# Clipping the up projections of 32 experts on ScalarE in two rectified steps instead of on VectorE in one

## What is computed

```
gate = xb @ w_gate[e] + b_gate[e]
up = xb @ w_up[e] + b_up[e]
gate = jnp.minimum(gate, 7.0)
up = jnp.clip(up, -7.0, 7.0)
glu = gate * jax.nn.sigmoid(1.702 * gate)
return (glu * (up + 1.0)) @ w_down[e] + b_down[e]
```

## Time and profile before

| | us |
|---|---|
| median of three runs | 1713.48 |
| lowest and highest of them | 1712.59, 1715.12 |
| profiled execution | 1710.51 |
| its span in the trace | 1709.2 |
| TensorE busy in it | 1615.4 (95%) |
| VectorE busy in it | 1343.9 (79%) |
| ScalarE busy in it | 1196.1 (70%) |

### The profile page before, as it was taken

How to read it: one execution, slowest core, us unless ns; L and a number is a source line. 1 busy time by engine, 2 the same in 40 slices (tenths; PEclk the granted TensorE clock), 3 DMA queues, 4 the chain that set the end, 5 groups by cost and what they waited for, 6 DMA issues and landing times.

```text
span 1709.2 us, 19409 instructions
## 1 busy us (share of the span) xinstructions
PE 1615.4 (95%) x7465; PEld 1304.9 (76%) x7465; DVE 1343.9 (79%) x1032; ACT 1196.1 (70%) x931; POOL 238.7 (14%) x169
## 2 busy tenths in 40 slices
PE   6999977999999999999999999999978999999998
PEld 5877865877877877877877877877865877778886
DVE  4476688899999999999999999999986325865343
ACT  4354356888888888888888888888865256664232
POOL 1402028131120120120120120120000000000000
PEclk9999989999999999999999999999997999999999
DMA  8412287999999999999999999999974311113221
GB/s 289 132 50 74 91 287 288 389 407 413 413 408 416 412 409 416 409 410 410 409 410 409 410 410 407 406 410 407 392 291 153 123 50 60 64 56 123 90 72 50
DMA packets 96335, 483.85 MB, mean 283 GB/s; under 512 B 14616, under 2 KB 16336, under 8 KB 47088
## 3 DMA queue, kind: packets, MB, share of 16 engines
q1 hardware_dynamic: 81408, 458.45, 67.0%
q0 software_dynamic: 10624, 18.35, 4.2%
q10 hardware_dynamic: 4208, 5.77, 1.0%
HBM read 475.91 MB, written 23.51 MB: 292 GB/s over the span
## 4 chain that ended last, share of the span: by engine, by line
PE 75%; DVE 13%; ACT 7%; issue 4%; DMA 1%; ACTq 0%; SPq 0%; DVEq 0%
PE PS L546 66%; ACT WH L1048 5%; DVE low L1401 4%; DVE WL L1401 4%; PE PS L788 3%; PE PS L983 1%; DVE eu L1747 1%; DVE eu L1752 1%; PE PS L995 1%; PE PS L802 1%; PE PS L578 1%; DVE hl L1738 1%; DMA h2d<-HV 1%; PE PS L658 0%; PE PS L976 0%
## 5 line engine op out<-in xcount | busy, mean ns | idle before, releaser
L1048 ACT ACTIVATE WH<-land 128x2048 fp32r<-128x2048 f32 x210 | 396.6, 1912 | 139.7 <-PE PS L546 138.9
L1048 ACT ACTIVATE WH<-ring 128x2048 fp32r<-128x2048 f32 x218 | 411.9, 1913 | 92.8 <-PE PS L546 84.5
L1401 DVE TENSOR_TENSOR low<-ring,WH 128x2048 fp32r<-128x2048 f32 x194 | 437.2, 2286 | 22.4 <-ACT WH L1048 21.4
L1401 DVE TENSOR_TENSOR WL<-land,WH 128x2048 fp32r<-128x2048 f32 x190 | 427.7, 2286 | 23.5 <-ACT WH L1048 22.9
L2072 POOL DMA_INDIRECT accd<-ys,lists x29 | 61.2, 2109 | 774.3 <-ACT ys L1236 774.3
L546 PE MATMUL PS<-WH,xh 128*128 128x512 f32 x512 | 161.0, 396 | 3.7 <-DVE low L1401 2.9
L546 PE MATMUL PS<-WH,hh 128*128 128x512 f32 x512 | 149.2, 393 | 1.5 <-DVE hh L1736 1.5
L546 PE MATMUL PS<-WH,xs 128*128 128x512 f32 x512 | 144.3, 405 | 1.8 <-DVE xs L1736 1.8
L546 PE MATMUL PS<-WH,xl 128*128 128x512 f32 x512 | 137.3, 390 | 0.0
L1401 DVE TENSOR_TENSOR WL<-ring,WH 128x2048 fp32r<-128x2048 f32 x24 | 54.8, 2289 | 92.9 <-ACT WH L1048 92.9
L546 PEld LDWEIGHTS PS<-WH,xs 128*128 128x128 f32 x512 | 98.2, 195 | 21.9 <-issue 2.2
(11 more groups left out here) (423 smaller groups left out, 2947.9 us busy)
## 6 DMA issues: line engine op xcount, KB each, us to landing
land<-in_w_up_dram SPq DMA_DIRECT2D x71, 1024.0 KB, 9.1
ring<-in_w_down_dram SPq DMA_DIRECT2D x71, 1024.0 KB, 9.5
ring<-in_w_gate_dram SPq DMA_DIRECT2D x66, 1024.0 KB, 9.6
land<-in_w_gate_dram SPq DMA_DIRECT2D x62, 1024.0 KB, 10.2
ring<-in_w_up_dram SPq DMA_DIRECT2D x57, 1024.0 KB, 9.2
land<-in_w_down_dram SPq DMA_DIRECT2D x57, 1024.0 KB, 10.0
ring<-in_w_in_dram SPq DMA_DIRECT2D x19, 1024.0 KB, 5.7
land<-in_w_in_dram SPq DMA_DIRECT2D x13, 1024.0 KB, 5.2
```

The source lines that it names most:

```text
L1048: A.activation(WH[buf[n]], lands[spot[n]], ACT.Copy).then_inc(s_hi, 1)
L1401: V.tensor_tensor(WLn[n], lands[spot[n]], WH[buf[n]].bitcast(F32), SUB).then_inc(s_lo, 1)
```

## The change

`vector_up` goes away for all experts. In its place stands `scalar_up`: ScalarE reads the up sums from PSUM and writes `eu = relu(7 - up)`, waits for its own result, and writes `eu = relu(14 - eu)`, which is the clipped up plus 7. VectorE's product adds -6 instead of 1. A constant column with 14 is added to the constants, in a column that the load of constants covered already.

The places in the queues change too. For even experts from 2 to 30, `scalar_up(e)` stands in the loop of e itself, at item d3, ahead of the high part of g3 of the next expert, and `vector_glu(e)` moves one item forward, to the place that `vector_up` had. For odd experts and for expert 0, `scalar_up` stands in the next loop at item g0, behind the high part of g4, and `vector_glu` stays at item g1. For the last expert, 31, `scalar_up` stands ahead of `scalar_out(30)` and of the last `hh`.

```diff
+    c[:, LIM], c[:, LIM2] = 7.0, 14.0
...
+    def scalar_up(e):
+        if small(e):
+            A.wait_ge(s_fold, fold["up", e])
+        else:
+            A.wait_ge(s_mm, done[n_g[e, 7] + 1])
+        if e:
+            A.wait_ge(s_tt, t_mid[e - 1] + 1)
+        A.activation(eu, PS[:, 2:4, :], ACT.Relu, scale=-1.0, bias=C[:, LIM:LIM + 1]).then_inc(ac.sem, ac.one())
+        A.wait_ge(ac.sem, ac.n)
+        A.activation(eu, eu, ACT.Relu, scale=-1.0, bias=C[:, LIM2:LIM2 + 1]).then_inc(s_eu, 1)
...
             if e == E:
+                scalar_up(E - 1)
                 scalar_out(E - 2)
...
+                if (what, p) == ("d", 3) and 0 < e < E and not small(e):
+                    scalar_up(e)
                 high(ahead(n_g[e, p] if what == "g" else n_d[e - 1, p]))
+                if (what, p) == ("g", 0) and e and (small(e - 1) or e == 1):
+                    scalar_up(e - 1)
...
-        V.tensor_scalar(eu, PS[:, 2:4, :], 7.0, -7.0, MIN, MAX).then_inc(s_eu, 1)
...
-        V.scalar_tensor_tensor(eu, eu, 1.0, eg, ADD, MUL).then_inc(s_eh, 1)
+        V.scalar_tensor_tensor(eu, eu, -6.0, eg, ADD, MUL).then_inc(s_eh, 1)
...
-                vector_up(E - 1)
                 vector_glu(E - 1)
...
-                if (what, p) == ("g", 0) and e:
-                    vector_up(e - 1)
-                if (what, p) == ("g", 1) and e:
+                if (what, p) == ("g", 1 if small(e - 1) or e == 1 else 0) and e:
                     vector_glu(e - 1)
```

More of the change, by code:

```diff
@@ L21 @@
 KB = 1024
-IDENT, LTRI, TRII, ONES, CAUS, SEL4, RCP, TOKK, IOTA, IOT1, OVJ, EPS5, EPS6, LIM = 0, 128, 256, 384, 512, 640, 1152, 1216, 1232, 1264, 1392, 1395, 1396, 1397
+IDENT, LTRI, TRII, ONES, CAUS, SEL4, RCP, TOKK, IOTA, IOT1, OVJ, EPS5, EPS6, LIM, LIM2 = 0, 128, 256, 384, 512, 640, 1152, 1216, 1232, 1264, 1392, 1395, 1396, 1397, 1398
 NC1 = 1400
@@ L51, in constants @@
     c[:, EPS5], c[:, EPS6] = 1e-5, 1e-6
-    c[:, LIM] = 7.0
+    c[:, LIM], c[:, LIM2] = 7.0, 14.0
     late = c[:, NC1:]
```

## The result

| | median us | runs | lowest, highest |
|---|---|---|---|
| before | 1713.03 | 4 | 1710.72, 1715.12 |
| after | 1723.80 | 4 | 1723.49, 1724.57 |

The changed kernel takes 1.0068 times as long as the one before, with a 95% interval of 1.0056 to 1.008: 10.8 us slower. The forecast was 1725.4 us, 11.9 us slower. The profiled execution took 1723.87 us, with a span of 1722.6.

What follows compares the result with a forecast made beforehand. TensorE, busy 95%, was taken to bound the kernel, waiting on the ScalarE and VectorE chain to the product and `hl`; +16.0 - 1.0 - 1.1 - 2.0 = +11.9 us gave 1725.4 us, range 1721 to 1730 (8 in 10: 1712 to 1735).

Steps and rivals of the forecast that it cites:

- The deciding term: Even experts 2 to 30: ScalarE's 2.20 us delay `hl`, less VectorE's 1.13; 1.07 us lost in each of 15 pairs, +16.0 us.
- Odd experts at no cost: Odd experts 1 to 29: `scalar_up` at g0 fits its 2.20 us into ScalarE's waits; cost nothing.
- The ends: Experts 0 and 31: VectorE's chain gets shorter at 0, ScalarE is free at 31; -1.0 and -1.1 us.
- The clock: TensorE's falls to half clock behind the transposes, in 7 of 15 pairs, mostly do not come; -2.0 us.
- The rival with more falls: Waits around d0: the clock falls behind the `hh` wait and costs fully, 1735 to 1739 us; chance 13%.
- The sum: Whole kernel: +16.0 - 1.0 - 1.1 - 2.0 = +11.9 us, giving 1725.4 us.
- Busy times: Sign in the changed trace: ScalarE busy some 72 us longer, VectorE 39 us shorter.

Runs made afterwards that it cites:

- one-step run: Changed kernel with the second rectified step left out for even experts 2 to 30 (outputs not the reference's); 1707.73 us against 1711.37, ratio 0.9977.
- one-item-later run: Changed kernel with the even experts' two steps one item later, behind the high part of g4; 1721.03 us against 1711.37, ratio 1.0049.
- x6: Changed kernel with `hh` directly behind `egl` and `hl` ahead of the low part of g6, in odd experts' loops; 1705.78 us against 1711.71, ratio 0.9964.
- x8: Kernel before, all clips still on VectorE, only reordered: product, `hh` and `hl` earlier; 1702.05 us, ratio 0.9945.
- x9: Order of x8, loading only half the columns of d1 and d3 of experts 1 to 31 (outputs not the reference's); 1682.14 us against 1712.11, ratio 0.983.

## Why the prediction was right

**The deciding term.** Forecast: +1.07 us in each of 15 pairs, from 2.20 added on ScalarE and 1.13 taken off VectorE. Measured in an undisturbed pair: 65.00 - 63.96 = 1.04. Each link is in the rows above: the steps cost 2.20 us, VectorE's low part of g4 begins 8.67 us behind the released piece (forecast 8.7), the product's wait is 0.56 (0.6), `hh` 1.67 (1.9), `hl` 1.25 (1.5). The two waits were forecast 0.2 too long each and the end of the chain not: the forecast counted TensorE's work by its steps, while a wait is counted from the end of the last matmuls, 0.16 us beyond their step (1.07 against 0.91), and the first matmuls behind a wait take 0.73 us instead of 0.62. The one-step run shows that the delay counts one for one; the run with `hl` earlier shows that the chain ends at `hl`.

**Odd experts at no cost.** Right: ScalarE's timeline behind the fold is

```profile
568.04 1.10 ACT L1234 ACTIVATE eu<-PS,C 128x1024 f32<-128x1024 f32 x1
...
571.23 5.52 ACT L1048 ACTIVATE WH<-ring 128x2048 fp32r<-128x2048 f32 x3
577.89 1.92 ACT L1048 ACTIVATE WH<-ring 128x2048 fp32r<-128x2048 f32 x1 [1.14 <-PE PS L546]
```

The waits between the three high parts are filled, and the 1.14 us ahead of the fourth is still whole, as in the earlier trace rows.

**The ends.** Forecast -1.0 and -1.1. The start gave -1.9 in the trace: the group of the earlier trace rows's kind behind the first even expert comes at 359.30 instead of 360.13, with 1.04 of that pair's loss in it. Of it 0.3 us come from ahead of the experts (VectorE is 0.29 earlier at 250 us). The clip's part is 0.7 and not 1.0: the product begins at 273.80 instead of 274.79, these 0.3 included, since VectorE now waits 0.34 us for ScalarE's high part. The other 0.9 us arise between 283 and 346 us, where the stretches of half clock lie otherwise (two, at 283 and 293 us, before; a double one at 288 us after). That part was not in the forecast and is luck. The tail gave -1.1: from the last such group (1193.71 and 1204.70) to the transposes of expert 31 it is 80.04 us before and 79.97 after, with the last pair's 1.04 in it.

**The clock.** Forecast -2.0, since the falls would go. Right: 7 became none. The reason given, that the waits would be shorter or set apart, is supported by the one-item-later run, where one wait grew to 2.33 us and the falls came in nearly every pair. The rival with more falls named a mechanism that exists, as that run shows, but it needed a wait longer than 1.67 us.

**The sum.** Up to the second block's transposes the trace gives 1318.73 - 1307.19 = +11.5 us, forecast +11.9. The 15 pairs gave 13.9 of it (14 x 0.92 and 1.04 for the last, the clock's gain included; forecast 14.0), the ends -3.0 (forecast -2.1), and 0.6 arose between the last expert and the second block, which the forecast did not have. The second block then was 1.9 us longer in this execution, by the fall of the clock described above, so the span grew by 13.4, and the medians by 10.8. The pairs are what the forecast had worked out; that the whole came out within 1.1 us is in part luck, as the small terms cancel and single executions of before differ by 4.4 us.

**Busy times.** By their group the 64 new instructions of ScalarE take 72.1 us, the forecast 72, but its busy time on the page grew by 60.8 and VectorE's fell by 34.9 (forecast 39), since the page counts overlaps once. That changes nothing in the sum, which went by steps of the queue.

**What was not seen.** I took it for granted that the weights leave room. For the change they do, but the orders that mend TensorE's waits run into them at 412 to 413 GB/s, 0.3 to 0.5 us a pair below where the kernel before stood.

## What to carry to other kernels

Price a moved instruction by its place in the receiving queue, not by that engine's busy share: the same two steps cost 2.20 us in a place where each following instruction was awaited, and nothing where the engine was going to wait for TensorE anyway. Before relieving an engine, ask whether an instruction in its queue can just be moved ahead of work that is not yet due; here this gave 16 us for one line, more than the 10.8 us that the choice of the engine had cost. And when one wait is mended, look at what is next in line (here the transfers, and for x6 still the two steps) before summing up what the rest would bring.

## What the runs showed of the hardware

**A wait of 1.7 us and one of 2.3 us are not alike.** Behind the first for `hh` TensorE's clock never fell (15 places), behind the second in 14 of 15; the fall then lengthened the next matmuls from 0.62 to 1.05 us for two. The length of the wait alone does not tell: behind 1.74 us for the product, with eight transposes next, it fell in 7 of 15 places of the kernel before.

**No order got the weights faster than 413 GB/s on this one core.** Before the change the transfers ran at 410 GB/s over that stretch and ScalarE never waited for weights; the order of x8, whose pairs take 62.1 us while landed weights last, takes 63.6 on the whole with 413 GB/s, and ScalarE waits. With fewer bytes its pairs take 62.1 us, all but one.

**GpSimd's instructions are longer where VectorE is busier, but not in step with it.** The windows from 500 to 1000 us, of before and of after (fifth number: GpSimd):

```profile
500.00:1000.00 500.00, 480.93 (x2232) 393.26 (x2231) 479.51 (x251) 438.57 (x289) 73.86 (x32) 0.99 1.01 410
```

```profile
500.00:1000.00 500.00, 474.98 (x2213) 384.97 (x2213) 454.79 (x231) 462.41 (x316) 54.26 (x31) 1.00 1.01 404
```

GpSimd issues the same gathers and scatters, two for each expert, in all of them. With VectorE busy 454.8 us of 500 they take 54.3 us, with 479.5 they take 73.9, and with 492.8 (x9, above) 156.1; but with 482.2 (x8, above) only 67.8. TensorE did not wait for a gather in this stretch. The Trainium skill, SBUF — State Buffer, section SBUF: two separate sides, tells of a port that VectorE and GpSimd share and one locks; most of the numbers go that way, but no run was made to test it.
